# Two transformer blocks on one Trainium2 core: products of three norms taken on unnormalised x, the final turn moved into the last down stage, and work buffers placed on a multiple of 64 bytes

## The reference

```python
def _rms_norm(x, gain, eps=NORM_EPS):
    y = xf * lax.rsqrt(jnp.mean(xf * xf, axis=-1, keepdims=True) + eps)
    return (y * gain.astype(jnp.float32)).astype(x.dtype)

def _conv_ffn(x, w_up, conv_w, conv_b, w_down):
    g, u = jnp.split(x @ w_up, 2, axis=-1)
    half = FFN_CONV // 2
    gp = jnp.pad(g, ((0, 0), (half, half), (0, 0)))
    gc = conv_b
    for j in range(FFN_CONV):
        gc = gc + conv_w[j] * gp[:, j:j + s]
    act = jax.nn.gelu(gc.astype(jnp.float32), approximate=False).astype(x.dtype)
    return (act * u) @ w_down

def second_block(...):
    for i in range(DEPTH_2):                       # 2 layers
        hn = _rms_norm(h, mix_norm[i])
        y = _pool_mixer(hn, ...) if i == 0 else _diff_attention(hn, ...)
        h = h + y
        h = h + _conv_ffn(_rms_norm(h, ffn_norm[i]), ...)
    return _rms_norm(h, final_norm)
```

## Time and profile before

| | us |
|---|---|
| median of 3 runs (lowest to highest) | 2436.46 (2435.92 to 2437.37) |
| the profiled execution | 2435.78 |
| its span, first to last instruction | 2434.1 |
| busy PE, DVE, ACT, POOL | 2255.2 (93%), 1309.9 (54%), 873.6 (36%), 641.5 (26%) |
| bytes moved, mean rate | 212.60 MB, 87 GB/s |

### The profile page before, as it was taken

The page is one execution under the profiler, slowest core; times in us unless marked ns, Lnnn a source line. Parts: engine busy times, 40 slices in busy tenths (PEclk is TensorE's granted clock), DMA queues, the critical chain, the costliest instruction groups (busy, mean ns, idle before and its releaser), DMA issues.

```text
span 2434.1 us, 31707 instructions
## 1 busy us (share of the span) xinstructions
PE 2255.2 (93%) x10796; PEld 1845.2 (76%) x10796; DVE 1309.9 (54%) x1766; ACT 873.6 (36%) x1291; POOL 641.5 (26%) x640
## 2 busy tenths in 40 slices
PE   5899999999889989999998999999888886999998
PEld 5688878888767868888887888887566654888887
DVE  6567665776643444344456544434777775544432
ACT  1323223232212223232224544422566663544421
POOL 3277667777750030000110000021123231000011
PEclk6899999999999999999998999999999997999999
DMA  6233333333323332333331333332111110333332
GB/s 215 78 104 96 86 90 103 95 90 90 100 61 95 95 87 83 98 95 93 95 108 41 107 95 96 94 95 78 53 52 52 52 52 18 104 100 98 91 95 65
DMA packets 351925, 212.60 MB, mean 87 GB/s; under 512 B 8520, under 2 KB 339714, under 8 KB 351747
## 3 DMA queue, kind: packets, MB, share of 16 engines
q1 hardware_dynamic: 343130, 185.82, 26.2%
q0 software_dynamic: 7680, 25.17, 3.5%
q10 hardware_dynamic: 1065, 0.96, 0.1%
HBM read 209.82 MB, written 2.10 MB: 87 GB/s over the span
## 4 chain that ended last, share of the span: by engine, by line
PE 73%; DVE 14%; issue 7%; ACT 4%; DMA 1%; POOL 1%; ACTq 0%; DVEq 0%; POOLq 0%; SPq 0%
PE ps L1866 21%; PE ps L1868 21%; PE ps L1867 21%; PE ps L2026 3%; PE ps L1893 2%; ACT at_swap L1027 2%; DVE w_lo L1118 1%; DVE small L1777 1%; DVE small L1447 1%; DVE gd_y_t L1421 1%; DVE gd_q_s L1308 1%; ACT w_hi L694 1%; DVE gd_q_g L1409 1%; PE ps L1975 1%; DMA ada<-w_ada 1%
## 5 line engine op out<-in xcount | busy, mean ns | idle before, releaser
L1866 PE MATMUL ps<-h_hi,w_hi 128*128 128x512 f32 x1896 | 775.4, 409 | 40.6 <-DVE gd_y_t L1421 8.9
L1118 DVE TENSOR_TENSOR w_lo<-raw,w_hi 128x1024 fp32r<-128x1024 f32 x335 | 439.1, 1312 | 587.2 <-ACT w_hi L694 586.1
L1868 PE MATMUL ps<-h_hi,w_lo 128*128 128x512 f32 x1896 | 752.7, 397 | 0.0
L1867 PE MATMUL ps<-h_lo,w_hi 128*128 128x512 f32 x1896 | 751.1, 396 | 0.0
L694 ACT ACTIVATE w_hi<-raw 128x1024 fp32r<-128x1024 f32 x335 | 354.3, 1058 | 716.2 <-PE ps L1868 669.2
L1866 PEld LDWEIGHTS ps<-h_hi,w_hi 128*128 128x128 f32 x1896 | 364.5, 192 | 114.2 <-issue 37.7
L1868 PEld LDWEIGHTS ps<-h_hi,w_lo 128*128 128x128 f32 x1896 | 363.2, 192 | 79.5
L1867 PEld LDWEIGHTS ps<-h_lo,w_hi 128*128 128x128 f32 x1896 | 364.9, 192 | 68.4
L551 POOL TENSOR_TENSOR sq_sum<-x 128x512 f32<-128x512 f32 x5 | 5.2, 1041 | 950.8 <-DVE x L1630 522.3
L1866 PE MATMUL ps<-act_hi,w_hi 128*128 128x512 f32 x528 | 208.8, 396 | 0.0
L1868 PE MATMUL ps<-act_hi,w_lo 128*128 128x512 f32 x528 | 208.8, 396 | 0.0
(11 more groups left out here) (339 smaller groups left out, 2932.9 us busy)
## 6 DMA issues: line engine op xcount, KB each, us to landing
raw<-ffn_w_up SPq DMA_DIRECT2D x88, 512.0 KB, 3.8
raw<-w_in SPq DMA_DIRECT2D x72, 512.0 KB, 3.8
raw<-w_ffn_in SPq DMA_DIRECT2D x44, 512.0 KB, 3.7
ada_w<-w_ada POOLq DMA_DIRECT2D x64, 256.0 KB, 3.4
raw<-ffn_w_down SPq DMA_DIRECT2D x32, 512.0 KB, 3.6
raw<-diff_w_qkv SPq DMA_DIRECT2D x24, 512.0 KB, 3.7
ada<-w_ada SPq DMA_DIRECT2D x4, 2048.0 KB, 15.3
ada_w<-w_ada_f POOLq DMA_DIRECT2D x32, 256.0 KB, 3.2
```

The source lines that it names most:

```text
L1118: nc.vector.tensor_tensor(w_lo[:, tile.slot], raw[:, tile.raw], w_hi[:, tile.slot].bitcast(F32), SUB)\
L1866: nc.tensor.matmul(dst, w_hi[:, tile.slot, k], hi, start=first, stop=False)
L1867: nc.tensor.matmul(dst, w_hi[:, tile.slot, k], lo, start=False, stop=False)
L1868: return nc.tensor.matmul(dst, w_lo[:, tile.slot, k], hi, start=False, stop=last)
```

## The change

Five edits.

1. `N_FFN0`, `N_ATT` and `N_FFN1` become late norms. ACT writes `h_hi` = x times gain (`unnormed_hi`), DVE `h_lo` = x times gain less `h_hi` (`unnormed_lo`), with no token factor. The products start on them; `sums` and the rows of the factor are put between the products of the first group (`late_norm`), and ACT copies the rows from bank 3 to `sq_tmp` (`keep_rows`).
2. The factor is applied behind the products. In the up loops DVE multiplies the gate's bank by `sq_tmp` into SBUF ahead of ACT's Identity, and the up bank by `sq_tmp` ahead of the product with gelu. In the attention the tables of cosine and sine are multiplied once, and v's bank is read by a DVE multiply instead of an ACT copy. For `N_ATT` the pieces of h are made inside the down stage of FFN1.
3. `POOLW` takes four banks in turn instead of two, and the third tile of `ATT_Q` bank 5 instead of 0.
4. In the last down stage ACT writes x times the final gain (`final_weighted`), PE turns tile m-1 behind the down product of tile m (`final_turn`) into banks 3 to 6, ACT empties the first four tiles (`first_half`), and the token factor is applied last, by DVE on one half of the features and by ACT on the other; SP writes 512 columns of 128 tokens in each of 8 DMAs.
5. The offset where the work buffers start is rounded up to a multiple of 64: 116576 becomes 116608 bytes of a partition. `sq_sum`, `sq_tmp`, `tmp`, `act_hi`, `act_lo`, `sc_hi`, `sc_lo` and the buffers of the heads move; `h_hi`, `h_lo`, `og_hi` and `og_lo` stay where they were, on multiples of 64.

```diff
@@ table of stages and buffers
-    POOLW = stream.stage(2, [5, 6] * 4)
+    POOLW = stream.stage(2, [5, 6, 0, 1] * 2)
-    ATT_Q = stream.stage(3, [0, 1, 0])
+    ATT_Q = stream.stage(3, [0, 1, 5])
-        work = place[0]
+        work = place[0] = (place[0] + 63) // 64 * 64
@@ SP, output
-            for m in range(KD):
-                sp.wait_ge(fin_act, m + 1)
-                sp.dma_start(out_t[:, :, m * P:m * P + P], o_tok[:, :, m * P:m * P + P]).then_inc(out_done, 16)
+            for n in range(NC):
+                for half, ready in enumerate((fin_dve, fin_act)):
+                    cs = slice(T * half, T * half + T)
+                    sp.wait_ge(ready, n + 1)
+                    sp.dma_start(out_t[:, n, cs], o_tok[:, n, cs]).then_inc(out_done, 16)
@@ ACT
-            def normed_hi(r):
-                for m in range(KD):
-                    act.wait_ge(n_ht, scaled_base(r) + m + 1)
-                    nc.scalar.activation(h_hi[:, m], tmp[:, 2 + m % 4], ACT.Copy).then_inc(n_hi, 1)
+            def unnormed_hi(r, gain, m):
+                nc.scalar.activation(h_hi[:, m], x[:, m], ACT.Copy, scale=col(vec, gain + m)).then_inc(n_hi, 1)
+            def keep_rows(r):
+                act.wait_ge(n_pe, 2 * r + 2)
+                nc.scalar.activation(sq_tmp[:], bank(3), ACT.Copy).then_inc(rows_out, 1)
+            def final_weighted(m):
+                if m >= 4:
+                    act.wait_ge(fin_pe, m - 3)
+                b, before = DOWN[2].out(m % 4, m // 4)
+                act.wait_ge(out_used[b], before + 1)
+                nc.scalar.activation(tmp[:, m % 4], x[:, m], ACT.Copy, scale=col(vec, V_FIN + m)).then_inc(fin_x, 1)
+            def first_half():
+                act.wait_ge(fin_pe, 4)
+                for n in range(NC):
+                    nc.scalar.activation(o_tok[:, n, 0:T], bank(3 + n), ACT.Copy).then_inc(fin_half, 1)
+            def second_half():
+                act.wait_ge(fin_pe, KD)
+                act.wait_ge(n_pool, N_OUT2 + 1)
+                for n in range(NC):
+                    nc.scalar.activation(o_tok[:, n, T:2 * T], bank(3 + n), ACT.Copy, scale=small[:, S_RSTD + n:S_RSTD + n + 1])\
+                      .then_inc(fin_act, 1)
@@ ACT, up loop, f > 0
-                            nc.scalar.activation(tmp[:, 2 + j], bank(b), ACT.Identity,
+                            split(UP[f].tile(2 * j, i).ahead())
+                            b, before = UP[f].out(2 * j, i)
+                            act.wait_ge(out_used[b], before + 1)
+                            nc.scalar.activation(tmp[:, 2 + j], tmp[:, j], ACT.Identity,
...
-                            act.wait_ge(out_used[b], before + 1)
+                            act.wait_ge(f_dve, 4 * i + (own + 2 * j + 2))
                             nc.scalar.activation(tmp[:, j], tmp[:, 2 + j], ACT.Gelu).then_inc(f_act, 1)
@@ ACT, last down stage
+                    if f == 2 and n % 3 == 2:
+                        final_weighted(m)
+                        if m == 5:
+                            first_half()
@@ DVE
+            def unnormed_lo(r, gain, m):
+                dve.wait_ge(n_hi, split_base(r) + m + 1)
+                nc.vector.scalar_tensor_tensor(h_lo[:, m], x[:, m], col(vec, gain + m), h_hi[:, m].bitcast(F32), MULT, SUB)\
+                  .then_inc(h_ready, 1)
@@ DVE, up loop, f > 0
+                            gs = tmp[:, j]
+                            nc.vector.tensor_tensor(gs, bank(b), sq_tmp[:], MULT).then_inc(out_used[b], 1)
...
+                            nc.vector.tensor_tensor(gu, bank(bu), sq_tmp[:], MULT).then_inc(out_used[bu], 1)
+                            dve.wait_ge(out_used[bu], before_u + 1)
                             dve.wait_ge(f_act, 4 * i + (base + 2 * j + 2))
-                            nc.vector.tensor_tensor(gu, tmp[:, j], bank(bu), MULT).then_inc(out_used[bu], 1)
+                            nc.vector.tensor_tensor(gu, tmp[:, j], gu, MULT).then_inc(f_gu, 1)
@@ DVE, attention
+            for name in ("cos", "sin"):
+                nc.vector.tensor_tensor(at[name][:], at[name][:], sq_tmp[:], MULT).then_inc(rope_rows, 1)
+            def v_tile(stage, t, j, i):
+                split(stage.tile(t, i).ahead())
+                b, before = stage.out(j, i)
+                dve.wait_ge(tile_done, stage.tile(t, i).before + 1)
+                nc.vector.tensor_tensor(at["v_f"][:], bank(b), sq_tmp[:], MULT).then_inc(out_used[b], 1)
@@ PE
-                product_group([(UP[f], t) for t in range(3)], h_hi, h_lo, (h_ready, split_base(r)), 5)
+                product_group([(UP[f], t) for t in range(3)], h_hi, h_lo, (h_ready, split_base(r)), 5,
+                              late_norm(r) if r in LATE_NORMS else None)
...
+                    for n in range(KD):
+                        down(n % 4, n // 4)
+                        if n:
+                            final_turn(n - 1)
+            def final_turn(m):
+                pe.wait_ge(fin_x, m + 1)
+                if m == 4:
+                    pe.wait_ge(fin_half, NC)
+                for n in range(NC):
+                    t = turn(part(bank(3 + n), m % 4), part(tmp[:, m % 4], n))
+                t.then_inc(fin_pe, 1)
```

More of the change, by code:

```diff
@@ L246, in block_kernel @@
     DVE_SUMS = (N_FFN0, N_FFN1)
-    SCALED_NORMS = (N_MIX, N_FFN, N_OUT1, N_FFN0, N_ATT, N_FFN1, N_OUT2)
+    SCALED_NORMS = (N_MIX, N_FFN, N_OUT1)
+    LATE_NORMS = (N_FFN0, N_ATT, N_FFN1)
     def split_base(r):
@@ L279, in block_kernel @@
         x = sb("x", [P, KD, T])
+        h_hi_at = place[0]
         h_hi = sb("h_hi", [P, KD, T], F32R)
@@ L1102, in _ @@
                 act.wait_ge(out_used[b], before + 1)
+                unnormed_hi(N_FFN1, V_FFN + KD, m)
                 square(N_FFN1, m)
             split(ATT_WO.tile(0, 0).ahead())
-            normed_hi(N_FFN1)
+            keep_rows(N_FFN1)
             feed_forward(2)
-            for m in range(KD):
-                output(m)
+            second_half()
         @block.vector
@@ L1726, in _ @@
                   .then_inc(out_used[b], 1)
-                if m >= 3:
-                    add_square(N_FFN0, m - 2)
-            add_square(N_FFN0, KD - 2)
-            normed_gain(N_FFN0, V_FFN, POOLW.tile(1, 0).ahead())
+            unnormed(N_FFN0, V_FFN, pooled_in, (POOLW.tile(1, 0).ahead(),))
+            dve.wait_ge(rows_out, 1)
             feed_forward(1)
-            normed_gain(N_ATT, V_MIX + KD, DOWN[1].tile(11, 1).ahead())
+            split(DOWN[1].tile(11, 1).ahead())
+            mean_squares(N_ATT)
             dve.wait_ge(lam_in_s, 64)
@@ L1762, in _ @@
             rope_tile(ATT_Q, 1, 1, 0, 1, "q")
-            split(ATT_Q.tile(2, 0).ahead())
+            v_tile(ATT_Q, 2, 2, 0)
             dve.wait_ge(rp_pe, 2)
@@ L1831, in att_head @@
                 if nxt:
-                    split(stage.tile(t0 + 2, i).ahead())
+                    v_tile(stage, t0 + 2, j0 + 2, i)
             att_head(ATT_0, 0, 0, False, True)
@@ L1911, in product_group @@
                 for n, (tile, b) in enumerate(pairs):
+                    if between is not None and n < 2:
+                        between(n)
                     for k in range(together, KD):
@@ L1950, in norm, with rows, late_norm @@
                     sums(r)
+                rows(r)
+            def rows(r):
                 pe.wait_ge(n_pool, r + 1)
                 rows_of(3, S_RSTD).then_inc(n_pe, 1)
+            def late_norm(r):
+                return lambda n: rows(r) if n else sums(r)
             pe.wait_ge(x_in, 16)
@@ L2214, in _ @@
             nc.tensor.matmul(bank(4), ones[32:33, :], pos_f[32:33, :], start=True, stop=True).then_inc(rp_pe, 1)
-            norm(N_FFN0)
             feed_forward(1, N_FFN0)
-            norm(N_ATT)
-            product_group(((ATT_Q, 0), (ATT_Q, 1)), h_hi, h_lo, (h_ready, split_base(N_ATT)))
+            product_group(((ATT_Q, 0), (ATT_Q, 1)), h_hi, h_lo, (h_ready, split_base(N_ATT)), 5, late_norm(N_ATT))
             product(ATT_Q, 2, 0, h_hi, h_lo)
@@ L2267, in att_head @@
                         open_out(stage.out(0, i))
+                        if stage is ATT_0:
+                            b, before = ATT_Q.out(2, 0)
+                            pe.wait_ge(out_used[b], before + 1)
                         for n in range(NC):
```

150 lines of the change are left out of this document (84 added, 66 removed).

## The result

The changed kernel takes 2446.01 us (median of 6 runs, 2436.67 to 2447.54) against 2436.38 (6 runs, 2430.42 to 2437.37): a ratio of 1.0037 with a 95% interval of 1.0019 to 1.0055. It is 0.4% slower; 2425.8 and faster was predicted, in a range that ended at 2440. The profiled execution's span is 2445.8, 11.7 more than before. One of the twelve executions of e3_v_first took 6872.85 and is left out of its ratio; all other executions here are in the same fast state.

What follows compares the result with a forecast made beforehand. PE was taken as the bound, with 73% of the span's chain. Terms -11.7 - 15.0 - 7 - 10.5 + 1 + 27.8 + 4.7 = -10.7 gave 2425.1 us profiled, 2425.8 as median; range 2398 to 2440.

Steps and rivals of the forecast that it cites:

- v_f on DVE: Attention heads: an ACT copy becomes a 0.68 us DVE multiply, mostly hidden by PE's slack; +1 us (0 to +2).
- The up loops: FFN1 and FFN2: serial ACT and DVE chain of 22.6 us per iteration against PE's 21.76; +27.8 us for both.
- The norms: Products start before the token factor at N_FFN0, N_ATT and N_FFN1: -15.0, -7 and -10.5 us.
- The alignment: Down stages and products on `sc`: work buffers on multiples of 64 save 6.6 ns per product; -11.7 us.
- rival D: Alignment is not the cause of the 0.2333 spacing, so its term is 0; 2437.5 us, no change; chance 0.13.
- Output: Last down stage and tail: transposes +2.8, PE gap and cold clock +5.5, shorter tail -3.6; sum +4.7 us.
- Ahead of the first band product: Stretch from the start to the first band product, predicted 4.8 us shorter.
- Rival B: Up loops: the chain stays under PE's period, 21.5 us or less per iteration; time 2398 us; chance 0.18.
- Rival C: Up loops: chain longer than the rows say; at 23.6 us per iteration, 2448 us; chance 0.15.
- The signs that the prediction names as showing it wrong: FFN1 and FFN2 loops taking PE's 21.76 us throughout, or the down stage's adds staying 15.40 us apart.

Runs made afterwards that it cites:

- e3_v_first: Changed kernel with v's multiply on DVE put ahead of the weight split in the attention heads; 2443.60 us, ratio 1.0046 to the kernel before.
- e6: Changed kernel with v copied by ACT, its token factor left out of the computation; 2436.12 us, ratio 1.0012 to the kernel before.
- e2: Changed kernel with both DVE row multiplies put ahead of the weight split in the up loops; 2412.79 us, ratio 0.9923 to the kernel before.
- e11: Changed kernel with only the up tile's row multiply ahead of the weight split in the up loops; 2415.79 us, ratio 0.9920 to the kernel before.
- e4: Changed kernel with ACT's copies of the first output half behind tile 4 instead of tile 5; 2439.40 us, ratio 1.0017 to the kernel before.
- e1: Kernel before with only the start of the work buffers rounded up to a multiple of 64; 2422.84 us against 2434.85, ratio 0.9962.
- e7: Changed kernel with the attention's norm done as before the change; 2443.95 us, ratio 1.0031 to the kernel before.
- e9: Changed kernel with the moves of e2 and e4, and the attention's norm done as before; 2403.63 us, ratio 0.9875 to the kernel before.
- e10: Changed kernel with the moves of e2 and e4, v copied by ACT and its factor applied by POOL; 2395.67 us, ratio 0.9846.
- e5: Changed kernel with the moves of e2, e3_v_first and e4 together; 2402.89 us, ratio 0.9867 to the kernel before.

## Why the prediction was wrong

The median came out 20 above the forecast. By the profiles the sum of -10.7 became +11.7, so 22.4 are to be found: 10.1 in the heads, 5 in the up loops, 5 in the norms, 2.4 ahead of the first band product and 0.2 in the output. By the prediction's own steps:

- **v_f on DVE, +1 (0 to +2): the step that failed most.** Measured +11.1 in the heads (they take 334.7 to 337.7 in the four kernels that have it as the changed one, 324.6 before), 8.8 of it gone in e6. I wrote "The heads have some slack on PE" and bounded the cost from PE. But the period of a head is set by DVE and ACT: in the kernels without this multiply on DVE it is 40.6 to 40.7 at a granted clock of 0.96 as at 1.00, and with it 41.5 at 0.96 and, in one head each of e2 and e11, at 1.00. That is 0.85 in each of 8 heads, some 7. The rest goes with heads at a granted clock of 0.92. Two heads of the changed kernel (span, PE, PEld, DVE, ACT and POOL busy, granted clock, DMA share, GB/s):

```profile
1787.90:1829.40 41.50, 35.35 (x164) 26.03 (x164) 29.84 (x46) 24.18 (x47) 11.50 (x9) 0.96 0.17 51
```

```profile
1829.40:1872.00 42.60, 36.93 (x164) 27.13 (x164) 29.40 (x46) 24.27 (x47) 11.58 (x9) 0.92 0.17 49
```

  41.5 at 0.96, and 42.6 at 0.92. Of the full heads of the four kernels with the multiply behind the split (changed, e2, e4, e11) 9 of 24 are at 0.92, with 42.6 to 43.4; of those of the six without it on DVE (before, e1, e6, e7, e9, e10) 2 of 36, with 41.4. Whether PE's longer waits bring the lower clock was not tried. I had looked at the page's shares, where DVE is 54% busy, and not at what ended PE's waits in the heads before: ACT and DVE nearly throughout, with 19.4 for `wo_s` and 8.6 for `at_q_lo` as the largest sums.
- **The up loops, +27.8: right in mechanism, 5 too small.** 22.75 per iteration against 22.6. PE lost 5.7 and 5.8 inside the loops, where I had none, because I let all of it fall on the third weight tile of the first down product; there it lost 10.8 and 10.5 more, 8.05 and 8.08 of them waiting for `act_lo` and the rest mostly on a cold clock behind it. Together 32.8; e2 gave back 33.2. So this step is the change's great loss, as forecast; what I did not weigh is how near the bound it lies (e11). One hop that no row had is seen now: ACT's Identity takes 0.816 from SBUF (mean of 44) and took 0.759 from psum. DVE's product takes 0.692 with both operands in SBUF and took 0.679 with one in psum. So of the two differences that the prediction quotes, ScalarE's shows here and VectorE's does not.
- **The norms, -15.0, -7 and -10.5: measured -11.3, -7.2 and -9.0.** The first is 3.7 short. At 1303.60 PE waits 1.83 for the first x and then runs cold:

```profile
1303.60 0.66 PE L1937 MATMUL ps<-h_hi,w_hi 128*128 128x512 f32 x1 [1.83 <-DVE x L1778]
1304.07 0.63 PE L1938 MATMUL ps<-h_lo,w_hi 128*128 128x512 f32 x1
1304.49 0.63 PE L1939 MATMUL ps<-h_hi,w_lo 128*128 128x512 f32 x1
```

  I had the products follow the position product without a gap and at full clock, and took the cold start as saved: 1.83 and 1.9 are the 3.7. In the third, 1.5 short, PE waits 1.16 for the last x.
- **The alignment, -11.7: right.** The stages of e1 make -11.5 (medians -12.0), and the spacing in the down stages is 0.2267 to the digit; on `sc` it is 0.229. The rule from the Trainium skill ("TensorE: Matmul & The Clock Gate", section "Wait — 56ns, not 53.3ns?"), columns/2.4 plus 2.5 ns and nothing for the address, does not describe this, and its 0.216 is below the aligned 0.2267 as well; rival D, which came from it, is out.
- **Output, +4.7: measured +4.9.** The turns cost 2.9 (e5, where the gap is gone), the gap behind the sixth down product and its cold clock 6.7, the tail -4.7.
- **Ahead of the first band product, -4.8: measured -2.4.** The only edit there is the alignment; the granted clock of that stretch is 0.962 for 0.964 before, and whether that is the whole of it was not tried.
- **Rival B** is out: the chain came out as the rows said. **Rival C** gave the sign and nearly the size, 2448, but not the mechanism, so by luck: the chain in the up loop was 0.15 and not 1 longer than the rows say, and the time lies in the heads and the norms. The signs that the prediction names as showing it wrong did not come; none of them looks at the heads.

## What to carry to other kernels

A stage in which PE is 87% busy (35.7 of 41 us in the heads before) can still be set by another engine's chain; before an operation is moved onto an engine, look at what ends PE's waits in that stage, and count the operation in full for each pass if it is that engine. Where an engine waits for its partner's half of a step, as DVE does for 1.54 and 1.65 in the up loops, an operation put ahead of that step is hidden, and put behind it counts in full: there the order of two instructions on DVE was worth 33 us, and that of one of them about as much. Where the wait is 0.17, as in the heads, the same move gave 2.4. When a wait is the first sign of lateness, taking that wait away only moves it; leave the work out once and see.

## What the runs showed of the hardware

In the down stages a 512-column product whose moving operand starts 32 bytes past a multiple of 64 takes 0.2333, on a multiple 0.2267 (e1). This is not the whole rule for the spacing. In the stage where `sc` and `og` take turns, a tile of 24 takes 5.50 on either once both are on multiples of 64, 0.229 each, so the 0.2288 of `og` in the earlier trace rows belongs to the stage and not to its address; why it is above 0.2267 there was not tried. In the heads the products on `at_ao_hi` and `at_ao_lo`, which moved by 32 bytes too, show no change (0.233 between neighbours before and in e1, at a granted clock of 1.00).

The other is how far a run moves with its granted clock. In the first block's heads all kernels here run the same instructions; the first product of the gate stage starts at 754.3 in the profile of e9 and at 769.2 in that of e4. The windows that end just ahead of it, e9 first:

```profile
40.00:750.00 710.00, 647.78 (x3681) 551.01 (x3682) 447.90 (x684) 202.67 (x366) 451.39 (x497) 0.97 0.32 91
```

```profile
40.00:766.00 726.00, 661.80 (x3686) 560.79 (x3687) 449.64 (x685) 203.24 (x366) 451.42 (x497) 0.95 0.31 89
```

Some 3,680 matmuls in both; 710 us at 0.97 and 726 at 0.95, with PE busy for 14.0 of the 16 more and DVE, ACT and POOL for the same time to 2 us. Single executions of one kernel lie up to 17 apart in the same way: of the twelve of e1 the fastest, 2413.5, had a mean granted clock of 0.970 and the slowest, 2430.7, 0.962, with the others between in both. So a profile's span alone would have misled by as much as the change is worth. Why the clock falls in one execution and not in another stays open; no run here was made for it.
